# Attentions with queries on partitions: the softmax's division put into the transposing matmul, by a diagonal matrix in place of the identity

## The reference, cut to what matters

```python
def _softmax_attend(q, k, v):                       # the other attentions are alike,
    s = einsum('bqhd,bkhd->bhqk', q, k) * scale     # with a bias, a mask or a sink
    p = softmax(s, axis=-1)
    return einsum('bhqk,bkhe->bqhe', p, v)

def _diff_attend(q, k, v, lam):
    s = einsum('bqhte,bkhte->bhtqk', q, k) * (q.shape[-1] ** -0.5)
    p = softmax(s, axis=-1)
    a = p[:, :, 0] - lam * p[:, :, 1]
    return einsum('bhqk,bkhe->bqhe', a, v)

def rmsnorm(x, g):
    return x * rsqrt(mean(x * x, axis=-1) + EPS) * g
```

## Time and profile before

| | |
|---|---|
| Median of 3 runs | 4693.87 us (4688.9 to 4701.96) |
| The profiled execution's own time | 4695.59 us |
| Span of the profiled execution | 4693.6 us |
| Granted clock of TensorE, mean | 0.887 |
| TensorE matmul (PE) busy | 3980.4 us, 85% |
| VectorE (DVE) busy | 2285.9 us, 49% |
| ScalarE (ACT) busy | 1443.7 us, 31% |
| GpSimd (POOL) busy | 422.7 us, 9% |

### The profile page before, as it was taken

One profiled execution on the slowest core, in us unless ns is written; L12 is line 12 of the kernel. 1 busy time (PEld: TensorE's weight loads), 2 busy tenths in 40 slices (PEclk: granted clock), 3 DMA queues, 4 the chain that ended last, 5 costly groups with the idle time before them and its releaser, 6 DMA issues. The chain is left out here.

```text
span 4693.6 us, 44440 instructions
## 1 busy us (share of the span) xinstructions
PE 3980.4 (85%) x18448; PEld 3113.2 (66%) x18448; DVE 2285.9 (49%) x3674; ACT 1443.7 (31%) x2369; POOL 422.7 (9%) x398
## 2 busy tenths in 40 slices
PE   4899987887979999996988888876879998787877
PEld 2688865555758888884766666654756776565556
DVE  4899246555642222235564454444444555333344
ACT  3221244443121111123453333333233444222231
POOL 2111100000010000001000212211010000000000
PEclk9899968887989999997998889876978997898878
DMA  2133230002401111112001000002200000000012
GB/s 77 59 108 122 105 116 20 23 17 97 163 32 47 45 43 48 46 49 72 30 20 35 14 15 14 20 15 82 74 31 27 22 26 14 27 6 8 8 57 87
DMA packets 67514, 225.23 MB, mean 48 GB/s; under 512 B 7848, under 2 KB 11944, under 8 KB 67312
## 3 DMA queue, kind: packets, MB, share of 16 engines
q1 hardware_dynamic: 43056, 132.68, 8.6%
q0 software_dynamic: 20800, 77.12, 4.6%
q10 hardware_dynamic: 3456, 12.58, 0.7%
HBM read 180.95 MB, written 37.74 MB: 47 GB/s over the span
## 5 line engine op out<-in xcount | busy, mean ns | idle before, releaser
L1954 PE MATMUL PS<-m,m 128*128 128x512 f32 (+4 forms) x4216 | 1751.5, 416 | 354.3 <-DVE m L2289 64.1
L1955 PE MATMUL PS<-m,m 128*128 128x512 f32 (+4 forms) x4216 | 1644.6, 391 | 0.0
L1956 PE MATMUL PS<-m,m 128*128 128x512 f32 (+4 forms) x4216 | 1640.9, 390 | 0.0
L1954 PEld LDWEIGHTS PS<-m,m 128*128 128x128 f32 (+1 forms) x4216 | 832.6, 198 | 734.6 <-issue 283.9
L1956 PEld LDWEIGHTS PS<-m,m 128*128 128x128 f32 (+1 forms) x4216 | 840.4, 200 | 157.0
L1955 PEld LDWEIGHTS PS<-m,m 128*128 128x128 f32 (+1 forms) x4216 | 843.7, 200 | 125.8 <-issue 2.9
L2550 DVE TENSOR_TENSOR m<-PS,m 128x512 fp32r<-128x512 f32 x352 | 240.6, 689 | 416.2 <-ACT m L2213 414.9
L2286 DVE TENSOR_TENSOR m<-m,m 128x1024 fp32r<-128x1024 f32 (+4 forms) x203 | 212.3, 1046 | 429.5 <-ACT m L2119 428.9
L2213 ACT CAST m<-PS 128x512 fp32r<-128x512 f32 x352 | 203.8, 584 | 363.3 <-PE PS L2041 362.9
L2041 PE MATMUL PS<-m,m 128*128 128x128 f32 x1408 | 251.5, 308 | 72.9 <-DVE m L2550 32.3
L2119 ACT CAST m<-m 128x1024 fp32r<-128x1024 f32 (+4 forms) x235 | 213.0, 907 | 249.8 <-PE PS L1956 188.7
(11 more groups left out here) (194 smaller groups left out, 3690.2 us busy)
## 6 DMA issues: line engine op xcount, KB each, us to landing
m<-in_w SPq DMA_DIRECT2D x220, 512.0 KB, 3.3
g_scratch<-m ACTq DMA_DIRECT2D x24, 512.0 KB, 2.8
m<-g_scratch POOLq DMA_DIRECT2D x24, 512.0 KB, 4.5
m<-in_w SPq DMA_DIRECT2D x32, 256.0 KB, 2.7
x_scratch<-m POOLq DMA_DIRECT2D x2, 4096.0 KB, 12.3
y_scratch<-m POOLq DMA_DIRECT2D x15, 512.0 KB, 2.9
m<-y_scratch POOLq DMA_DIRECT2D x15, 512.0 KB, 5.1
y_scratch<-m POOLq DMA_DIRECT2D x7, 640.0 KB, 3.2
```

The costliest lines, as they stand in the source:

```text
L1954: pe.e.engine.matmul(o, L[0], X[0], start=start, stop=False)
L1955: pe.e.engine.matmul(o, L[0], X[1], start=False, stop=False)
L1956: return pe.e.engine.matmul(o, L[1], X[0], start=False, stop=stop)
```

## The change

The full multiplication of `E` goes. In its place the identity is multiplied with the column of reciprocals, which gives a diagonal matrix (`diag`, 128x128, four buffers), and `turn` is a plain matmul of the block of `E` with this diagonal: out[k, q] = sum over p of E[p, k] * diag[p, q] = E[q, k] / sum[q]. In the differential attention the first map isn't divided either: the second is multiplied with -lam * sum0 / sum1 and added, and the diagonal holds 1 / sum0. GpSimd's part of `soft3` goes.

The norms use only the matrix of 1/1024, and the square root gets a scale of 4 or 8 where 1/256 or 1/128 stood; 256 columns of constants and their load go. Three small buffers (`mw`, `mc`, `mm`) and `m3` stand elsewhere in the layout.

```diff
@@ class Attention
         self.sums = [mem([P, 8]) for _ in range(4 + second)]
+        self.diag = [mem([P, P]) for _ in range(4)]
@@ soft1
         f["E"], f["sums"] = E, sums
+        if not k:
+            f["diag"] = self.diag[e][:, :]
@@ soft3
         if "first" in f:
-            f0 = f["first"]
-            f["from_first"] = f0["ready"]
-            f0["ready"] = [(self.S.norm, f["n"])]
+            f["first"]["ready"] = [(self.S.norm, f["n"])]
             self.e_free[f["e"]] = [(self.S.norm, f["n"])]
-        elif f.get("lam"):
-            f["ready"] = [(self.S.scaled, f["n"])]
-        else:
-            spans = []
...
-            f["spans"] = [E[:, c0:c1] for c0, c1 in spans]
+        elif not f.get("lam"):
             f["ready"] = [(self.S.norm, f["n"])] + [(self.S.pad, f["n"])] * bool(f["pad_at"])
@@ turn_over
-            blocks = [f["E"][:, e0:e0 + 128] for e0, _, _ in groups[g] for f in fr]
+            blocks = [(f["E"][:, e0:e0 + 128], f["diag"]) for e0, _, _ in groups[g] for f in fr]
@@ tensor_program, turn
-            for i, x in enumerate(s["blocks"]):
-                m = e.transpose(PS[:, s["out"] + 128 * i:s["out"] + 128 * i + 128], x, ident)
+            for i, (x, diag) in enumerate(s["blocks"]):
+                m = e.matmul(PS[:, s["out"] + 128 * i:s["out"] + 128 * i + 128], x, diag, start=True, stop=True)
@@ scalar_program, root
-            e.activation(s["rs"], s["ps"], ACT.Sqrt, bias=s["eps"]).then_inc(*act.says(S.root, n))
+            e.activation(s["rs"], s["ps"], ACT.Sqrt, bias=s["eps"], scale=s["scale"]).then_inc(*act.says(S.root, n))
@@ vector_program, soft3
+            if f.get("lam") and "first" not in f:
+                continue
             e.reciprocal(rs, total).then_inc(*dve.says(S.norm, (n, "recip")))
+            dve.wait_ge(S.norm, (n, "recip"))
             if "first" in f:
+                f0 = f["first"]
                 k = f["softs"][0][1].shape[1]
-                a, b = f["first"]["E"][:, 0:k], E[:, 0:k]
-                dve.wait_ge(S.norm, (n, "recip"))
-                e.tensor_scalar(rs, rs, p.lam_t[:, 1:2], None, ALU.mult).then_inc(*dve.says(S.norm, (n, "lam")))
+                a, b, s0 = f0["E"][:, 0:k], E[:, 0:k], f0["sums"]
+                dve.wait_ge(S.exp, f0["n"])
+                e.tensor_scalar(rs, rs, s0[:, 3:4], p.lam_t[:, 1:2], ALU.mult, ALU.mult).then_inc(*dve.says(S.norm, (n, "lam")))
+                e.reciprocal(s0[:, 6:7], s0[:, 3:4]).then_inc(*dve.says(S.norm, (n, "first")))
                 dve.wait_ge(S.norm, (n, "lam"))
-                for ev in f["from_first"]:
-                    dve.wait_ge(*ev)
-                e.scalar_tensor_tensor(out=a, in0=b, scalar=rs, in1=a, op0=ALU.mult, op1=ALU.add).then_inc(*dve.says(S.norm, n))
-            elif not f.get("lam"):
-                dve.wait_ge(S.norm, (n, "recip"))
-                for x in f["spans"]:
-                    m = e.tensor_scalar(x, x, rs, None, ALU.mult)
-                m.then_inc(*dve.says(S.norm, n))
+                e.scalar_tensor_tensor(out=a, in0=b, scalar=rs, in1=a, op0=ALU.mult, op1=ALU.add).then_inc(*dve.says(S.norm, (n, "sum")))
+                dve.wait_ge(S.norm, (n, "first"))
+                e.tensor_scalar(f0["diag"], ident, s0[:, 6:7], None, ALU.mult).then_inc(*dve.says(S.norm, n))
+            else:
+                e.tensor_scalar(f["diag"], ident, rs, None, ALU.mult).then_inc(*dve.says(S.norm, n))
@@ gpsimd_program
-        elif s.kind == "soft3":
...
-                e.tensor_scalar(f["E"][:, 0:k], f["E"][:, 0:k], f["sums"][:, 6:7], None,
-                                ALU.mult).then_inc(*pool.says(S.scaled, f["n"]))
```

More of the change, by code:

```diff
@@ L83 @@
         ("qn_g", 2), ("kvn_g", 1), ("fin_g", 8), ("cond", 16), ("blam", 256)]
-CONSTS = [("ident", 128), ("o1024", 128), ("o64", 128), ("o256", 128), ("o128", 128), ("swap32", 128),
+CONSTS = [("ident", 128), ("o1024", 128), ("o64", 128), ("swap32", 128),
           ("win", 384), ("col", 64)]
@@ L212 @@
            "lo", "sumsq", "recip", "scale", "rot", "addx", "merge", "max", "norm", "score", "topk", "lru", "bias", "outd",
-           "lo_g", "cos", "pad", "scaled", "colmask", "outg"]
+           "lo_g", "cos", "pad", "colmask", "outg"]
 MOVES, GATE_STORES, RING = 12, 4, 6
@@ L224, in __init__ @@
          self.topk, self.lru, self.bias, self.outd,
-         self.lo_g, self.cos, self.pad, self.scaled, self.colmask, self.outg) = self.all
+         self.lo_g, self.cos, self.pad, self.colmask, self.outg) = self.all
         self.move = [Signal(nc, f"move{n}", 16) for n in range(MOVES)]
@@ L864, in mean, with root, norm_split @@
         return (S.mean, n)
-    def root(rs, ps, b, done):
+    def root(rs, ps, b, done, scale=1.0):
         n = p.id()
-        p.add("root", n=n, rs=rs, ps=ps, after=done, eps=epst[0:rs.shape[0], 0:1])
+        p.add("root", n=n, rs=rs, ps=ps, scale=scale, after=done, eps=epst[0:rs.shape[0], 0:1])
         bank_free[b] = [(S.root, n)]
         return (S.recip, n)
-    def norm_split(src, kt, ones, chunks, g, shift, ready, hi, lo, bufs, sums=None):
+    def norm_split(src, kt, scale, chunks, g, shift, ready, hi, lo, bufs, sums=None):
         sq, rs, tmp = bufs
@@ L882, in norm_split @@
             o = bank(b)[:, 0:tn]
-            means.append((b, o, mean(o, ones, rs[c][:, 0:tn], sums.t[c], b)))
-        root_t = [root(rs[c][:, 0:tn], means[c][1], means[c][0], means[c][2]) for c, (t0, tn) in enumerate(chunks)]
+            means.append((b, o, mean(o, cc("o1024"), rs[c][:, 0:tn], sums.t[c], b)))
+        root_t = [root(rs[c][:, 0:tn], means[c][1], means[c][0], means[c][2], scale) for c, (t0, tn) in enumerate(chunks)]
         n, out_events, tmp_free = 0, {}, [[] for _ in tmp]
@@ L1416, in schedule @@
         pe_ = mem([P, 128])
+        m3 = mem([P, 3, 128], R)
+        mw, mc, mm = (mem([P, 20]) for _ in range(3))
         zq_at = mem.at
@@ L1422, in schedule @@
         qh, ql = mem([P, TC], R), mem([P, TC], R)
-        m3 = mem([P, 3, 128], R)
-        mw, mc, mm = (mem([P, 20]) for _ in range(3))
         with mem.over(v_at):
@@ L1584, in schedule @@
         inner_at = mem.at
-        mem([P, 11136])
+        mem([P, 11616])
         z_at = mem.at
@@ L1652, in finish_steps @@
                     b = take(banks)
-                    m = mean(bank(b)[:, 0:tn], cc("o128"), r, [(S.square, n)], b)
-                    t = root(r, bank(b)[:, 0:tn], b, m)
+                    m = mean(bank(b)[:, 0:tn], cc("o1024"), r, [(S.square, n)], b)
+                    t = root(r, bank(b)[:, 0:tn], b, m, 8.0)
                     p.add("subln", n=(h, c), y=yc, g8=g8[:, 0:1], r=r, z=zg[:, t0:t0 + tn], after=[t, (S.gateact, h)])
@@ L2268, in vector_program @@
 def vector_program(dve, p):
-    S, e = p.S, dve.e.engine
+    S, e, ident = p.S, dve.e.engine, p.ident
     for s in p.steps:
@@ L2679, in gpsimd_program @@
                 m.then_inc(*pool.says(S.pad, f["n"]))
-        elif s.kind == "soft3":
-            f = s["f"]
-            if f.get("lam") and "first" not in f:
-                k = f["softs"][0][1].shape[1]
-                pool.wait_ge(S.norm, (f["n"], "recip"))
-                e.tensor_scalar(f["E"][:, 0:k], f["E"][:, 0:k], f["sums"][:, 6:7], None,
-                                ALU.mult).then_inc(*pool.says(S.scaled, f["n"]))
         elif s.kind == "colmask":
@@ L2769, in constants @@
     p = np.arange(P)
-    out = {"ident": np.eye(P)}
-    for n in (1024, 256, 128):
-        out[f"o{n}"] = np.full((P, P), 1.0 / n)
+    out = {"ident": np.eye(P), "o1024": np.full((P, P), 1.0 / 1024)}
     out["o64"] = (p[:, None] // 64 == p[None, :] // 64) / 64.0
```

15 lines of the change are left out of this document (5 added, 10 removed).

## The result

The changed kernel takes 4751.01 us (median of 4 runs, 4747.41 to 4756.51), the kernel before 4692.14 in the same rounds: a ratio of 1.0123, with a 95% interval of 1.0103 to 1.0143. It is slower by some 58 us where I had forecast no change and a range up to 4716.

What follows compares the result with a forecast made beforehand. TensorE was taken to bound the kernel, busy for 3980.4 of 4693.6 us. VectorE's gain (-17), the differential stage's cost (+5) and TensorE's cost (+9) made -3 us off the median 4693.9: 4691, no change, range 4666 to 4716.

Steps and rivals of the forecast that it cites:

- the price of the plain matmul: TensorE's 1408 turning blocks: a plain fp32 matmul costs 0 to 13 us more in all than transposes; 5 taken.
- a cost on TensorE: Plain matmuls and longer weight loads in the turning groups, less some 3 us given back: 9 us, from 3 to 35.
- the argument for the clock: From 2759.0 to 2762.4, eight transposes and two matmuls ran and the clock then rose, so transposes count as busy.
- The rule that I set aside: Skill page's four times faster FP32 transpose, applied to the 1408 blocks: some 700 us more; rejected from the trace.
- my 7 us: Longer weight loads in the turning groups, exposed where TensorE had been idle: a third of the groups at 0.06 us.
- slower, by the weight loads: Rival: each of 1408 plain fp32 loads is exposed, 70 to 148 us: 4765 or more; mildest 4708; chance 0.10.
- The terms of the sum: VectorE gain -17 us, differential-stage cost +5, TensorE cost +9; VectorE's busy sum some 52 us lower, GpSimd's 120.
- The direct waits on the diagonal: TensorE's waits for the scaling's successor, 31.4 us before, were to be shorter by about 10.
- its -17 and +5: VectorE's shorter queue gains 17 us (7 to 32); diagonal and second reciprocal in the differential attention cost 5 (0 to 18).
- its wait for the exponential: TensorE's wait before the next scores in the differential attention, 45.2 us over 37 places, was to rise above that.
- a tenth of the half-clock time back as a rival: Shorter waits return a tenth of 567 us at 1.2 GHz to full clock, saving 28 us: 4663, chance 0.20.
- What I had set up to catch the error: Signs: transposing line's mean above 330 ns, scaling's successor well over 0.3 us, stage clocks moving over 0.02 without the waits.

Runs made afterwards that it cites:

- doubled transposes: The kernel before, with each transpose issued twice in a row onto the same place: 4764.25 us, ratio 1.0119.
- identity kernel: The kernel before, scalings kept, each transpose written as a plain matmul with the identity: 4753.28 us, ratio 1.010; once more, 4756.66 us, ratio 1.0114.
- the two fp32r kernels: The changed kernel with exponentials and diagonal written as fp32r, their matmul issued once (4735.31 us, ratio 1.0059) or twice (4861.03 us, ratio 1.0336).
- the one-pass kernel: The changed kernel with exponentials and diagonal written as fp32r, so their product is one fp32r matmul issued once: 4735.31 us, ratio 1.0059.

## Why the prediction was wrong

**The step that failed** is the price of the plain matmul: "1408 x 9 = 13 us, is the upper end; 0 is the lower, because the transpose's 273 may already be the same two passes. I take 5." It is 1408 second records, 162.5 us with all that their loads expose, against a cost on TensorE of "9 us, from 3 to 35". (That upper end was also added up wrongly: 13 for the matmuls and 35 for the loads, less 3, are 45.) The row that would have told was in my hands. I read L2027's 32 records as 32 matmuls. The program has 16 there, four times four; the order of TensorE's program before, cut to that line:

```
1839 L2027 MATMUL PS<-m_121,m_110 128x512 x4
1846 L2027 MATMUL PS<-m_121,m_110 128x512 x4
1853 L2027 MATMUL PS<-m_121,m_110 128x512 x4
1860 L2027 MATMUL PS<-m_121,m_110 128x512 x4
```

and the timeline of the same kernel:

```profile
577.27 5.67 PE L2027 MATMUL PS<-m,m 128*128 128x512 f32 x8
...
602.70 6.61 PE L2027 MATMUL PS<-m,m 128*128 128x512 f32 x8
```

Eight records for four instructions; and of the 32 records only every second one raises the semaphore that each of these matmuls raises. The transposing line had 1408 for 1408. That comparison gives the second record for each block; priced at the transposes' pace, near 110 ns each, it is 155 us.

The pace was there as well. At full clock the records of L2027 start 429 ns apart over 512 columns, so 107 ns for 128, and two of them are 215 ns, where the transposes start 109 ns apart (median). The difference, 106 ns, gives 149 us for 1408 blocks. I had compared durations, 592 and 273 ns, which hold a part that overlaps the next record. The same misreading stands in the argument for the clock: the "two matmuls" beside the eight transposes are the two records of one matmul over 256 columns.

**The rule that I set aside.** The page "TensorE: Matmul & The Clock Gate" of the Trainium skill speaks of a transpose mode four times faster for FP32. I rejected it with the 592 ns record, which was half an instruction. Its size is not borne out here, a block takes two records for one and some 225 ns for 110, a factor of two; its direction was right. The Trainium skill's page "FP8 and Floating Point Precision", in TensorE Precision Notes, says that true FP32 takes four passes; the runs agree with it in so far as a plain float32 matmul has two records here, each of which streams 128 columns in more time than fp32r does (270 ns at the least for 218).

**The weight loads.** Their length was right, 192 for 141 ns, and my 7 us for what of it is exposed was of the right order: doubled transposes with loads of 140 ns have groups 14 us shorter. The rival "slower, by the weight loads" had a time near the measured one, 4765 for 4751, by luck: it was the second record, not a load that fails to run beside the matmul before it.

**VectorE.** The terms of the sum held: 200 products of 296 and 306 ns, 59.7 us for the 57 forecast, VectorE 52.0 us less, GpSimd 121.7 less. The direct waits on the diagonal were to be 10 us shorter; they are 12 shorter with transposes in place (19.8 for 31.4) and 16 in the changed kernel. The gain of 12 us was measured at 15 to 33 alone, and in idle time its -17 and +5 came out as -14.3 and +5.9.

**The differential stage.** I had expected its wait for the exponential above 45.2 us; it is 43.2 in the changed kernel:

```profile
PE PS L1946 <- ACT m L2194: 43.2, 33, 7.4
```

With transposes in the same kernel it is 48.0 in 38 places. The identity kernel, which has the long groups and not the added work, has in the same window:

```profile
PE PS L1954 <- ACT m L2202: 40.0, 32, 7.4
```

So the long groups take 5 us off this wait, and the added work on VectorE puts 3 us on it with or without them. It is not hidden; the two effects have opposite signs, and I had forecast only the second. This stage came out even, +0.9 us, though its 84 groups cost 38.7; the identity kernel came out at -8.2 there.

**The clock.** I gave a tenth of the half-clock time back as a rival, 28 us. It came, at twice that size or more, as part of a loss: 63.8 us, and 88.9 in the second profile. I had named shorter waits as its cause. With the doubled transposes it came from more work on TensorE, and useless work at that. Less idle time by itself does not bring it: the two fp32r kernels had 40.4 and 74.3 us less of it and a lower clock. From the stage clocks, the time at 1.2 GHz fell from 567 to about 420 us (0.20 x 405 + 0.26 x 650 + 0.10 x 510 + 0.30 x 400); over the whole span, from 2 x 0.113 x 4693.6 = 1061 to 2 x 0.093 x 4745.8 = 883 us.

**What I had set up to catch the error** would have missed it: I named a mean above 330 ns for the line, and it is 294. A duration says nothing on a doubled count. The stage clocks did move by more than the 0.02 that I had named, but so did the waits.

## What to carry to other kernels

Before an instruction changes its form, count the records of the nearest line of that form against the instructions that the program issues there. The same 128x128 block cost one record as a float32 transpose and two as a plain float32 matmul, 115 ns more, and 1408 of them outweighed a saving of 52 us on an engine that was half idle. Work taken from a second engine is better moved to a third that nobody waits for (ratio 0.9939 here) than to the one that sets the end. And where a kernel runs partly at 1.2 GHz, price an edit on TensorE by the clock too: two thirds of this one's cost came back in idle time and clock, so a trial that looks cheap may hide much added work. Where one column of such a count moves by 25 us between two profiles of one kernel, profile twice before a gain of that size is given a cause.

## What the hardware showed that I had not expected

A plain float32 matmul runs as two records, each with its own 128x128 weight load (2816 for 1408 here, 32 for 16 in L2027). At full clock the records of 128 columns start 109 to 113 ns apart (medians from the traces) whether they are float32 transposes, the records of a plain float32 matmul or fp32r matmuls. For this shape, with a new load each, an fp32r record was no faster in the median than a float32 one, and an fp32r matmul has half as many. The pace had two sources: in float32 the next load ran beside the record from 2 ns on, in fp32r load and record took turns, 52 and 60 ns.

The granted clock was lower where the matmuls of the turning line streamed faster. With as many records, the kernel whose records take 270 ns at the least had 0.907, and the one whose records take 218 ns had 0.874; with half the records it was 0.869, under the 0.887 of the transposes. In the one-pass kernel that was worth as much as the waits themselves: +41.6 us on matmuls that nobody had changed, for -40.4 of idle time. It rests on these two pairs of kernels, which differ in other places too (the order of load and record, the pads' filling on GpSimd); a run with the speed of the columns as the only difference was not made, and the cause stays open.
